# Two more of the first block's projections by Strassen products, two fewer plain blocks in and after attention

## What is computed

```python
h = rms_norm(x, norm_gain[layer])
proj = jnp.einsum('bsd,dc->bsc', h, w_in[layer])
(sb_q, sb_k, sb_v, sb_g, r_q, r_k, r_v, r_g, m_sb, m_ret) = jnp.split(proj, SPLIT_POINTS, axis=-1)
out_a = merge_heads(stick_breaking_attention(qa, ka, va)) * jax.nn.silu(sb_g)
...
p_a = jnp.einsum('bsw,wd->bsd', out_a, w_branch_sb[layer])
p_b = jnp.einsum('bsw,wd->bsd', out_b, w_branch_ret[layer])
merged = (jax.nn.sigmoid(m_sb + b_merge[layer, 0]) * p_a
          + jax.nn.sigmoid(m_ret + b_merge[layer, 1]) * p_b)
x = x + jnp.einsum('bsd,de->bse', merged, w_out[layer])
```

## Time and profile before

| | |
|---|---|
| median of three runs | 2443.21 us |
| the profiled execution's own time | 2444.54 us |
| its span | 2442.7 us |
| PE busy | 2405.7 us, 98% of the span |
| DVE busy | 1614.6 us, 66% |
| ACT busy | 1030.8 us, 42% |
| POOL busy | 239.6 us, 10% |
| granted clock of TensorE | 0.999 |
| first attention score to the end of attention | 748.7 to 968.1 us |
| covering blocks | 968.1 to 1006.2 us |
| B1 to B1 + 3 | 1006.7 to 1098 us |

### The profile page before, as it was taken

The page is one execution under the profiler, slowest core; times in us unless marked ns, Lnnn a source line. Parts: engine busy times, 40 slices in busy tenths (PEclk is TensorE's granted clock), DMA queues, the critical chain, the costliest instruction groups (busy, mean ns, idle before and its releaser), DMA issues.

```text
span 2442.7 us, 30594 instructions
## 1 busy us (share of the span) xinstructions
PE 2405.7 (98%) x12042; PEld 1972.9 (81%) x12042; DVE 1614.6 (66%) x2079; ACT 1030.8 (42%) x1751; POOL 239.6 (10%) x395
## 2 busy tenths in 40 slices
PE   7999999999999999999999999999999999999998
PEld 6788888888887777889888877887888888888887
DVE  8777556556655766477742655167567776789889
ACT  6665322223335655223412346234545444533334
POOL 1011111111110000100010003000001211100000
PEclk9999999999999999999999999999999999999999
DMA  4222333333334222625233410110333444674433
GB/s 149 95 104 104 96 120 104 104 104 108 108 111 144 95 95 83 247 101 191 74 107 101 130 35 20 36 36 18 107 131 121 162 149 155 241 258 144 155 121 121
DMA packets 141775, 285.90 MB, mean 117 GB/s; under 512 B 18470, under 2 KB 91744, under 8 KB 134848
## 3 DMA queue, kind: packets, MB, share of 16 engines
q1 hardware_dynamic: 109168, 175.45, 21.7%
q0 software_dynamic: 32464, 108.49, 12.5%
HBM read 200.02 MB, written 83.89 MB: 116 GB/s over the span
## 4 chain that ended last, share of the span: by engine, by line
PE 87%; DVE 6%; ACT 2%; DMA 2%; DVEq 1%; issue 1%; ACTq 0%; SPq 0%; POOL 0%
PE ps L2781 37%; PE ps L620 12%; PE ps L3462 8%; PE ps L3045 6%; PE ps L2840 2%; PE ps L2859 2%; PE ps L614 2%; PE ps L3352 2%; PE ps L2887 2%; PE ps L2868 1%; PE ps L3337 1%; PE ps L2960 1%; PE ps L2975 1%; PE ps L3030 1%; DMA hidden_raw<-hidden_forms 1%
## 5 line engine op out<-in xcount | busy, mean ns | idle before, releaser
L1992 DVE TENSOR_TENSOR proj_out<-ps,proj_out 128x512 f32<-128x512 f32 x334 | 223.7, 686 | 256.9 <-PE ps L2781 243.3
L2781 PE MATMUL ps<-a_hi,pw_hi 128*128 128x512 f32 x600 | 235.0, 392 | 0.0
L2781 PE MATMUL ps<-a_lo,pw_hi 128*128 128x512 f32 x600 | 233.6, 389 | 0.0
L2781 PE MATMUL ps<-t_hi,pw_hi 128*128 128x512 f32 x560 | 220.4, 394 | 0.1
L2781 PE MATMUL ps<-t_lo,pw_hi 128*128 128x512 f32 x560 | 218.6, 390 | 0.0
L2781 PE MATMUL ps<-a_hi,pw_lo 128*128 128x512 f32 x400 | 155.8, 390 | 0.0
L2781 PEld LDWEIGHTS ps<-a_lo,pw_hi 128*128 128x128 f32 x600 | 112.7, 188 | 23.0
L2781 PEld LDWEIGHTS ps<-a_hi,pw_hi 128*128 128x128 f32 x600 | 112.7, 188 | 23.0
L1917 DVE TENSOR_TENSOR pw_lo<-pw_raw,pw_hi 128x512 fp32r<-128x512 f32 x200 | 128.5, 684 | 0.1
L1263 ACT ACTIVATE pw_hi<-pw_raw 128x512 fp32r<-128x512 f32 x150 | 83.6, 621 | 104.2 <-DMA pw_raw<-in_w_in 59.6
L2781 PEld LDWEIGHTS ps<-t_hi,pw_hi 128*128 128x128 f32 x560 | 105.4, 188 | 22.1 <-issue 0.5
(11 more groups left out here) (531 smaller groups left out, 6188.2 us busy)
## 6 DMA issues: line engine op xcount, KB each, us to landing
pw_raw<-in_w_in SPq DMA_DIRECT2D x36, 1024.0 KB, 6.0
projections<-proj_out POOLq DMA_DIRECT2D x112, 256.0 KB, 3.2
hidden_raw<-hidden_forms SPq DMA_DIRECT2D x28, 1024.0 KB, 4.8
pw_raw<-in_w_ff SPq DMA_DIRECT2D x16, 1024.0 KB, 6.1
w_quarter<-in_w_ff SPq DMA_DIRECT2D x16, 1024.0 KB, 7.0
hidden_forms<-proj_out POOLq DMA_DIRECT2D x56, 256.0 KB, 3.1
hidden_forms<-nb POOLq DMA_DIRECT2D x56, 256.0 KB, 3.4
w_raw<-in_w_in SPq DMA_DIRECT2D x10, 1024.0 KB, 5.2
```

The costliest lines, as they stand in the source:

```text
L1992: return dve.tensor_tensor(out_ap(n, j), product_bank(n, o), src, ALU.add)
L2781: last = pe.matmul(product_bank(n, o), w, a[:, k0 + k, t], start=(k == 0 and g == 0), stop=(k == 3 and g == 2))
```

## The change

`NPROJ` goes from 36 to 38. The third of the four blocks of each merge gate moves from the plain blocks to the Strassen blocks (`content`, `proj_kind`, `proj_column` follow). There are now one background block `L1` (slot 0) and one covering block `COVER` (slot 1); all later block numbers fall by two. Attention computes 4 outputs of `L1`, one in each pair of heads, and one of `COVER` in the last pair: 24, 24, 24 and 48 passes in place of 48, 48, 48 and 72. After attention three outputs of `COVER` are left in place of seven. Every background output is stored by POOL as before, and there are half as many.

```diff
-        NPROJ = 36
+        NPROJ = 38
...
-        FILL_PASSES = [(14, 2, 2, 2, 2, 2, 4, 2, 2, 3, 2, 3, 2, 2, 2, 2)] * 3 + [(14, 2, 2, 2, 2, 2, 5, 5, 4, 5, 5, 0, 2, 2, 4, 6)]
+        FILL_PASSES = [(6, 1, 1, 1, 1, 1, 2, 1, 1, 2, 1, 1, 1, 2, 1, 1)] * 3 + [(6, 2, 2, 2, 2, 2, 2, 2, 2, 2, 0, 2, 2, 2, 2, 4)]
...
-        COVER_ORDER = ((3, 0, 1, 2), (0, 1, 2, 3))
+        COVER_ORDER = (3, 0, 1, 2)
...
-        L1, COVER, B1, B2, L5 = 0, 2, 4, 8, 12
+        L1, COVER, B1, B2, L5 = 0, 1, 2, 6, 10
...
-            for s in range(2):
-                load_block(sp, COVER + s, s, w1_d[:, :, 9, (2 + s) * BC:(3 + s) * BC])
+            load_block(sp, B1, 0, wbs_d[:, :, 0:BC])
...
             for h in range(2):
                 sp.dma_start(decay[h][:, :], tab["decay"][h]).then_inc(const_in, 16)
-            load_block(sp, B1, 0, wbs_d[:, :, 0:BC])
             load_block(sp, B1 + 1, 1, wbs_d[:, :, BC:2 * BC])
...
             act.wait_ge(gated, 4 * 4 + 4)
-            split_hi(act, COVER + 1, 1)
             for k in range(KT):
                 act.activation(S_hi[:, k, :], OUT[:, k, :], ACT.Copy).then_inc(s_hi, 1)
             gate_from_store(0, 0, 1)
-            for s in range(2):
-                for v, j in enumerate(COVER_ORDER[s]):
...
-                split_hi(act, B1 + s, s)
+            for v, j in enumerate(COVER_ORDER):
+                act.wait_ge(gp_done, done(COVER, v))
+                act.wait_ge(pa_stored[j % 2], 16 * (2 + v // 2))
+                act.activation(stage[j % 2][:, :], bank[j], ACT.Sigmoid, bias=merge_bias(1, 3, j)).then_inc(kept[j], 1)
+                if v == 1:
+                    split_hi(act, B1, 0)
+            split_hi(act, B1 + 1, 1)
...
-            split_lo(dve, COVER + 1, 1)
             branch_low(0, range(KT))
             split_lo(dve, B1, 0)
...
-            gemm(pe, COVER, 0, A_hi, A_lo, False, outputs=(0, 1, 2))
-            gemm(pe, COVER + 1, 1, A_hi, A_lo, False)
+            gemm(pe, COVER, 1, A_hi, A_lo, False, outputs=(0, 1, 2))
```

More of the change, by code:

```diff
@@ L729, in proj_kind @@
         def proj_kind(n):
-            return "plain" if n == 0 else "norm" if n < 9 else "turn" if n < 13 or 20 <= n < 24 else "plain" if n < 26 else "silu" if n < 34 else "sigmoid"
+            return "plain" if n == 0 else "norm" if n < 9 else "turn" if n < 13 or 20 <= n < 24 else "plain" if n < 27 else "silu" if n < 35 else "sigmoid"
         def content(n):
-            return 12 if n == 0 else n - 1 if n < 13 else n if n < 24 else n + 10 if n < 26 else n - 2 if n < 30 else n if n < 34 else n - 6
+            return 12 if n == 0 else n - 1 if n < 13 else n if n < 24 else n + 11 if n < 27 else n - 3 if n < 31 else n if n < 35 else n - 7
         def proj_column(n):
@@ L805, in form_stored @@
             if name == "a11":
-                return (pa_stored[0], 16 * 8 + two) if b % 2 else (c_stored[0], 16 * 28 + two)
+                return (pa_stored[0], 16 * 4 + two) if b % 2 else (c_stored[0], 16 * 30 + two)
             if name == "a22":
-                return c_stored[1], 16 * 28 + 16 * (b + 1)
+                return c_stored[1], 16 * 30 + 16 * (b + 1)
             if name in ("a12", "s3"):
-                return c_stored[(2 if name == "a12" else 4) + n % 2], 16 * 14 + two
+                return c_stored[(2 if name == "a12" else 4) + n % 2], 16 * 15 + two
             q = ("s1", "s2", "s4").index(name)
@@ L1125, in _ @@
                 gate_again(proj_d[SB_MERGE].rearrange("p (c t) -> p c t", c=2), 0, j)
-            for b in range(2):
-                for j in COVER_ORDER[b]:
-                    th, ct = j // 2, j % 2
-                    pool.wait_ge(kept[j], kept_by(COVER + b))
-                    pool.dma_start(mr_d[:, 2 * b + ct, th * HALF:(th + 1) * HALF], stage[j % 2][:, :]).then_inc(pa_stored[j % 2], 16)
+            for j in COVER_ORDER:
+                th, ct = j // 2, j % 2
+                pool.wait_ge(kept[j], kept_by(COVER))
+                pool.dma_start(mr_d[:, ct, th * HALF:(th + 1) * HALF], stage[j % 2][:, :]).then_inc(pa_stored[j % 2], 16)
             for b in range(3):
@@ L1347, in gate_bias @@
             def gate_bias(n, ct):
-                c = COLS["merge"] + 8 + 2 * (n - 34) + ct
-                return cols[:, c:c + 1] if n >= 34 else 0.0
+                c = COLS["merge"] + 8 + 2 * (n - 35) + ct
+                return cols[:, c:c + 1] if n >= 35 else 0.0
             def proj_second(n, j):
@@ L1456, in sb_pair @@
                     if S - 1 in fill_after[i]:
-                        keep_filler(fill_after[i][S - 1])
-                    if i % 2 and S in (4, 5):
-                        half_hi(n + 1, (n + 1) % 2, S - 4)
+                        keep_filler()
+                    if i == 1 and S in (4, 5):
+                        half_hi(COVER, 1, S - 4)
                     if i < 3 or S < 14:
@@ L2041, in end_of_pair @@
                 dve.wait_ge(o_kept, 8 * i + 8)
-                for j in range(4) if i % 2 else ():
+                for j in range(4) if i == 3 else ():
                     dve.sem_inc(kept[j], 1)
@@ L2073, in sb_pair @@
                         weights(S)
-                    if i % 2 and S in (6, 7):
-                        half_lo(n + 1, (n + 1) % 2, S - 6)
+                    if i == 1 and S in (6, 7):
+                        half_lo(COVER, 1, S - 6)
                     if i < 3 or S < 15:
```

86 lines of the change are left out of this document (38 added, 48 removed).

## The result

The changed kernel takes **2452.26 us**, median of six executions (2449.34 to 2454.45), against 2443.25 for the kernel before (six executions, 2442.97 to 2444.19): the ratio is 1.0035, with a 95% interval from 1.0025 to 1.0045. It is slower by 9.0 us. The forecast was 2449.0, in a range from 2442 to 2454.

What follows compares the result with a forecast made beforehand. PE's own order was taken to set the pace. -5.4 for passes, +7.7 lost in attention and +3.5 at the handover gave +5.8 on the profiled 2444.54 us, 2450.3; forecast for the median 2449.0 us, range 2442.0 to 2454.0.

Steps and rivals of the forecast that it cites:

- rival 3: Handover loads: at 358 GB/s the third decay lands at 1008 and the handover costs 7 us: 2452.5 us; chance 0.12.
- The sum on PE: Whole kernel: 168 passes added, 96 fewer in attention and 96 in the covering gemm, net -24 at 0.227 us: -5.4 us.
- The start: Attention's start: turn(1) stays where it was with fewer passes ahead, so PE idles longer and 2.0 us are lost.
- Steps 2 and 3: Attention: turn(2) meets ACT's copy, turn(3) DVE's multiplication; 0.4 us lost in each of the first three pairs, 1.2 us.
- Step 11: Attention: ACT's chain after step 12's scores holds turn(11); three passes lost in each of four pairs, 2.7 us.
- Step 14: Attention: ACT's sigmoid and DVE's multiplication hold turn(14); 0.45 us lost in each of four pairs, 1.8 us.
- Rival 1: Attention: copies and scans move forward with the scores, only the start's 2.0 us is lost: 2443.3 us; chance 0.18.
- The handover: After attention: PE waits 1.5 us at B1, and B1+2's low part, behind the third decay, is late: 3.5 us altogether.
- Rival 2: Handover: the third decay lands by 1001.0, B1+2's low part is in time, only 1.5 us stays: 2447.0 us; chance 0.12.
- Rival 4: Attention's start: PE's clock falls to 1.2 GHz for as long as the 3.2 us stop, costing 1.6: 2450.6 us; chance 0.08.

Runs made afterwards that it cites:

- run 1: Changed kernel with the first pair's 24 background passes dealt anew, 14 at attention's start and at most one in each later step: 2449.36 us, ratio 1.0024.
- run 5: Kernel before with the first pair's 48 passes dealt anew, 6 at the start in place of 14, 8 moved to steps 7 to 11: 2445.79 us, ratio 1.0010.
- changed again: A second profile of the changed kernel, nothing edited: an execution of 2452.18 us, span 2450.4.
- run 6: Changed kernel with 12 spare passes on PE ahead of turn(1) of the first pair, result unread: 2449.95 us, ratio 1.0026.
- run 9: The kernel of run 8 with the pass tables of run 1 (first pair) and run 2 (second and third pairs): 2448.82 us, ratio 1.0018.
- run 8: Changed kernel with the third decay table loaded earlier, and ACT reading gates back after two covering outputs and B1's split: 2448.64 us, ratio 1.0020.
- run 4: Changed kernel with 8 spare passes on PE between B1 and B1+1, result unread: 2450.76 us, ratio 1.0030.
- run 2: Changed kernel with steps 11 and 14 given 3 passes each in pairs 1 to 3, taken from steps 6, 9, 10 and 13: 2450.44 us, ratio 1.0030.

## Why the prediction was right, and where it was not

The time lies within the range, and slower by over 0.2% was the likeliest of the three outcomes, at 0.50. It is 3.3 us above the forecast and just outside the forecast's own range of 2446 to 2452. It is also almost the number of rival 3 (2452.5), whose mechanism the trace doesn't bear out. By its steps:

- **The sum on PE, -5.4.** The two blocks moved the first score by 38.09 us, from 748.66 to 786.75, which is 168 passes at 0.227. Right.
- **The start, 2.0.** 3.19 us idle in place of 1.13: 2.06. Right; runs 1 and 5 show its cause and its size.
- **Steps 2 and 3, 1.2.** Too high: 0.22 at `turn(2)` in each of three pairs, nothing at `turn(3)`: 0.7.
- **Step 11, 2.7.** 0.90 in place of 0.20 in three pairs and 0.94 in place of 0.26 in the last: 2.8. Right.
- **Step 14, 1.8.** 0.59, 0.58 and 0.58 in place of two that are too short for the view to list and 0.48, and in the last pair 0.96 in place of 0.49: at most 1.7. Right. These four terms add up to 7.3, the difference of 10.2 and 2.9, but by the landmarks 6.6 us were lost in attention at full clock, against 7.7; where the other 0.7 went is open, but for the two short waits. Rival 1, with a loss of 2.0, falls.
- **The handover, 3.5.** The mechanism was right to the link: the first product is released by `decay`, which I put 36 us after attention's end, and it ran at 1029.29, 38.2 after 991.08. From the landing of `decay` at 1029.1 to the low part of `B1 + 2` it took 26.9 us, where I had 27.1. The size was not: 4.2 us in changed again (1.20, 1.88, 1.11). I had 1.5 at the start of `B1`, nothing at `B1 + 1`, and 2.0 at `B1 + 2`. The step of the handover that failed is "two outputs, the split for `B1 + 1`" as a mere link of the line to `B1 + 2`: PE wants that split too, after only one block of 21.8 us, and at full clock PE stood still for 1.8 to 2.0 us there. Rival 2 falls: PE stood still at `B1 + 1` in all six traces that keep the change's SP queue.
- **Rival 3, a slower queue.** Two stretches of the changed kernel's handover:

```profile
1007.00:1011.00 4.00, 2.82 (x13) 2.04 (x12) 1.65 (x1) 0.00 (x0) 0.00 (x0) 1.00 0.99 372
1011.00:1015.00 4.00, 4.00 (x20) 3.29 (x19) 0.00 (x0) 1.38 (x2) 0.72 (x2) 1.00 1.03 423
```

  Over the six such stretches from 1007 to 1031 us it is 372 to 423 GB/s, 402 on average, some 5% less than the 422 that I used, and the `decay` lands 1.6 us later than I put it (38.0 us after attention's end, against 36.4; the rival needed 40). The 358 GB/s of the Trainium skill, "DMA: Bandwidth & Descriptors", Specifications and Bandwidth, is passed in each of them. So the rival's number came near the result by other terms than its own.
- **Rival 4, the clock.** This is the term that I left out of the sum and gave 0.08. It is part of the typical execution: 206.64 - 204.33 = 2.3 us between two profiles of one program, and 2.3 to 2.65 us in the medians when PE is kept busy (run 6), not all of it surely the clock's. I had priced it at 1.6. This is the largest term that the sum lacks. The Trainium skill, "TensorE: Matmul & The Clock Gate", Part 1, has the array fall to half rate after an idle stretch; the traces agree in that each fall past 700 us stands at a stop of PE, but after 3.13 us it was 0.50 and after 3.19 us 1.00. The same part calls the count of slow matmuls at a kernel's start variable from run to run; here it varies in mid-kernel too. My error was to take one profile with a clock of 1.00, in which no stop was longer than 1.13 us, as evidence about one of 3.2.

With measured sizes the sum is -5.4 + 6.6 + 2.3 + 4.2 = +7.7. That is 1.9 us more than the forecast's +5.8, and is the span of changed again. The 9.0 of the medians is 1.3 more than that because the profiled execution of before, from which 7.7 is counted, lay 1.3 us above its own median, and changed again lies at the median of its kernel.

That the forecast was not further off is in part luck: attention was put 1.1 us too dear, which made up for a good third of the 3.0 us by which clock and handover together were too cheap. The range held because its upper end had 3.3 us in reserve for the handover and 1.8 for attention, not because it had the clock in it.

## What to carry to other kernels

Work that is taken out of an engine at 98% is worth its time only where nothing else keeps a time of its own. List the waits that the chain shows, count for each what stands ahead of it, and most of the loss can be summed in advance: here the sum had 11.2 us of losses, and changed again has 13.2. Where cover becomes shorter, follow each thing that the next stage needs block by block, not only the last one; in an in-order queue move loads that hang on one event ahead of waits for another. And where PE will stand still for longer than any stop of the trace, price the clock as part of the forecast.

## What the runs showed of the hardware

- Whether the granted clock falls after a stop of PE differs between executions of one program. At `turn(1)` stops of 3.19, 3.20 and 3.27 us were followed by a clock of 1.00, stops of 3.13, 3.42, 3.63 and 3.95 us by 0.50, and a stop of 2.44 us (run 5) by 1.00. At `B1 + 1` it fell after 2.04 and 1.97 us, and not after 2.00, 1.88 and 1.79. It fell after 1.87 us at another place (run 5) and after 2.94 us, but not 2.19, at `B1 + 2` (runs 9 and 8). So in these traces the length of the stop alone doesn't decide it.
- SP's issue of one load can itself take long. The load of `rq` behind five loads of 1 MB took 7.81 us to issue in the changed kernel, and 7.18 to 7.93 in the ten other traces with that order of loads, against 0.43 for the load of `rq1`, of the same size, second in the queue. All that stands behind it on SP is issued later by that; no run tells what this alone costs.
- A stretch at the lower clock can cost less than its passes say. Seven passes at half the clock made the block `B1 + 1` 1.6 us longer (23.5 us from its first pass to that of `B1 + 2`, against 21.9) and hid a wait of 1.2 us (run 4). From `B1` to the end it took 1431.68 and 1431.99 us in the changed kernel and run 6, where the clock fell at `B1 + 1`, and 1431.82 to 1432.29 in changed again, 1, 2 and 4, where it didn't.
